# Copying attention probabilities and the last residual into fp32r buffers by DMA, and transposing them as fp32r

## What is computed

```python
# first block: 8 heads of 64, window 128, blocks of 128 tokens
probs = softmax(concat([scores * 64 ** -0.5 + mask, sink]))[..., :-1]
out = einsum("bnhgqk,bnkhd->bnqhd", probs, vw)
# second block, two layers: 8 heads of 64, chunks of 64, 8 chunks to the left
p = softmax(where(valid, scores + bias, -1e30))
out = einsum("bnhqk,bnkhd->bnqhd", p, vb)
# end: the residual stream x plus the last projection, normalised
return rms_norm_2(x + y @ w_out, final_gain)
```

## Time and profile before

| | |
|---|---|
| Median of three runs | 1216.86 us |
| The profiled execution, its own time | 1217.13 us |
| Its span (first to last instruction) | 1215.0 us |
| PE busy | 1202.1 us, 99% |
| PEld busy | 1012.2 us, 83% |
| DVE busy | 827.8 us, 68% |
| ACT busy | 553.6 us, 46% |
| POOL busy | 385.8 us, 32% |

### The profile page before, as it was taken

How to read it: one execution, slowest core, us unless ns; L and a number is a source line. 1 busy time by engine, 2 the same in 40 slices (tenths; PEclk the granted TensorE clock), 3 DMA queues, 4 the chain that set the end, 5 groups by cost and what they waited for, 6 DMA issues and landing times.

```text
span 1215.0 us, 15012 instructions
## 1 busy us (share of the span) xinstructions
PE 1202.1 (99%) x5822; PEld 1012.2 (83%) x5822; DVE 827.8 (68%) x1520; ACT 553.6 (46%) x954; POOL 385.8 (32%) x283
## 2 busy tenths in 40 slices
PE   9999999999999999999999999999999999999997
PEld 7888888888888888888888879898888889898886
DVE  5868735466888537653569877767967866677864
ACT  6557533324444324433334566653335555643433
POOL 0035279997000000000003238775203033464200
PEclk9999999999999999999999999999999999999999
DMA  8232232322323232233223333222223332222221
GB/s 303 75 101 70 70 114 87 104 78 95 104 87 119 90 99 89 90 112 96 93 73 96 121 112 95 89 88 78 78 72 101 105 105 88 87 90 95 76 70 70
DMA packets 35911, 117.42 MB, mean 97 GB/s; under 512 B 3968, under 2 KB 4480, under 8 KB 35840
## 3 DMA queue, kind: packets, MB, share of 16 engines
q1 hardware_dynamic: 35552, 116.28, 29.6%
q10 hardware_dynamic: 288, 0.18, 0.0%
HBM read 114.35 MB, written 2.10 MB: 96 GB/s over the span
## 4 chain that ended last, share of the span: by engine, by line
PE 87%; DVE 7%; ACT 3%; issue 1%; POOL 1%; DMA 0%; SPq 0%; ACTq 0%; DVEq 0%
PE ps L284 84%; DVE RA L261 3%; DVE FA L273 2%; ACT RA L253 2%; PE ps L1415 1%; DVE FA L261 1%; POOL RA L261 1%; DVE RA L273 1%; PE ps L813 1%; ACT RA L257 1%; DMA FA<-w_units 0%; PE ps L479 0%; ACT FA L257 0%; PE ps L521 0%; POOL FA L261 0%
## 5 line engine op out<-in xcount | busy, mean ns | idle before, releaser
L284 PE MATMUL ps<-RA 128*128 128x512 f32 (+1 forms) x5470 | 1179.3, 376 | 6.4 <-DVE RA L261 4.1
L284 PEld LDWEIGHTS ps<-RA 128*128 128x128 f32 x5470 | 974.3, 189 | 188.9 <-DVE RA L261 4.8
L253 ACT ACTIVATE RA<-FA 128x1024 fp32r<-128x1024 f32 (+4 forms) x337 | 279.7, 857 | 338.7 <-PE ps L284 165.2
L261 DVE TENSOR_TENSOR RA<-FA,RA 128x1024 fp32r<-128x1024 f32 (+6 forms) x302 | 322.3, 1078 | 161.7 <-ACT RA L253 157.5
L261 POOL TENSOR_TENSOR FA<-FA 128x512 f32<-128x512 f32 (+1 forms) x88 | 116.4, 1324 | 443.3 <-ACT FA L257 417.3
L277 POOL TENSOR_SCALAR FA<-FA 128x256 f32<-128x256 f32 (+3 forms) x117 | 147.2, 1270 | 161.9 <-DVE FA L281 160.8
L273 DVE SCALAR_TENSOR_TENSOR FA<-ps,FA 128x512 f32<-128x512 f32 (+3 forms) x137 | 98.1, 721 | 90.2 <-PE ps L284 44.9
L261 POOL TENSOR_TENSOR RA<-FA,RA 128x512 fp32r<-128x512 f32 (+1 forms) x37 | 70.4, 1914 | 111.2 <-ACT RA L253 111.2
L258 ACT ACTIVATE FA<-FA 128x512 f32<-128x512 f32 (+4 forms) x109 | 60.3, 555 | 97.1 <-DVE FA L1385 76.0
L273 DVE SCALAR_TENSOR_TENSOR FA<-FA 128x4 f32<-128x4 f32 (+4 forms) x166 | 84.4, 515 | 20.6 <-ACT FA L253 7.9
L257 ACT ACTIVATE FA<-ps,FA 128x512 f32<-128x512 f32 x56 | 38.1, 684 | 108.3 <-PE ps L284 108.3
(11 more groups left out here) (43 smaller groups left out, 274.9 us busy)
## 6 DMA issues: line engine op xcount, KB each, us to landing
FA<-w_units SPq DMA_DIRECT2D x189, 512.0 KB, 3.5
FA<-rel SPq DMA_DIRECT2D x16, 256.0 KB, 3.2
FA<-w_units SPq DMA_DIRECT2D x8, 384.0 KB, 3.0
FA<-x SPq DMA_DIRECT2D x8, 256.0 KB, 5.7
FA<-x_rows SPq DMA_DIRECT2D x4, 512.0 KB, 9.2
FA<-dmat SPq DMA_DIRECT2D x8, 256.0 KB, 3.3
out<-FA SPq DMA_DIRECT2D x8, 256.0 KB, 2.2
FA<-w_units SPq DMA_DIRECT2D x2, 256.0 KB, 4.2
```

Source lines behind the costliest of these rows:

```text
L253: return lambda eng: eng.activation(dst, src, ACT.Copy)
L261: return lambda eng: eng.tensor_tensor(dst, a, b, op)
L284: return lambda e: e.matmul(dst, a, b, start=start, stop=stop_)
```

## The change

The 248 transposes of lines 813, 1415 and 1628 get operands and results of type fp32r, while the data keep their bits:

- A new buffer `UA` holds an identity of type fp32r (`identr`, one ACT copy) and 1280 columns `TP` for probabilities.
- First block: after `pn.s.3` a DMA `pm.s` on SP's queue copies the stage's probabilities from `P1` to a new double buffer `PR` in `RA` (128x1024, 512 KB; in stages 0 and 1 128x4x128, 256 KB). The transposes wait for the copy, and the probabilities' buffer is free from the copy on.
- Second block: after the two `pn` of a half a DMA copies its 640 columns (320 KB) to `TP`, and the five transposes wait for that.
- End: four DMAs `hm.t` copy the residual of 128 tokens each (128x8x128, 512 KB in pieces of 512 bytes) into unused places of `RA`. They are issued after units 1 to 4, and their transposes come after units 4 to 7.
- The early gate tiles move to other columns of `FA`, which makes room.

```diff
+        def turn(dst, src):
+
+            return lambda e: e.transpose(dst.bitcast(F32R), src, U(TI, 128))
...
+            a_move(s)
+
+        def a_move(s):
+
+            n, g = stages[s]
+            nk = 256 if n else 128
+            cut = lambda ap: steps(ap, [[256, 4], [1, nk]])
+            dma(f"pm.{s}", [f"pn.{s}.3"] + take(f"pr.{s % 2}"), cut(Rf(PR + 1024 * (s % 2), 1)),
+                cut(F(P1 + 1024 * (s % 2), 1)), f"pm{s % 2}")
+            for t in range(4):
+                free(f"p1.{s % 2}.{t}", f"pm.{s}")
...
-                    after = [f"pn.{s}.3"] + take(f"bank{b}") if t == 0 else []
-                    T(f"pT.{s}.{j}" if t == 3 else None, after, lambda e, t=t, j=j, b=b: e.transpose(
-                        bank(b, 128, 128 * t), F(pb + 256 * t + 128 * j, 128), F(ID, 128)))
...
+                    after = [f"pm.{s}", "identr"] + take(f"bank{b}") if t == 0 else []
+                    T(f"pT.{s}.{j}" if t == 3 else None, after,
+                      turn(bank(b, 128, 128 * t), R(pr + 256 * t + 128 * j, 128)))
...
+                    dma(f"{pre}pm.{h}.{half}", [f"{pre}pn.{h}.{i}" for i in pair] + take(f"tp{half}"),
+                        U(TP + 640 * half, 640).bitcast(F32), F(PB + 640 * half, 640), f"pm{half}")
+                    for i in pair:
+                        free(f"pb{i}", f"{pre}pm.{h}.{half}")
...
+                        after = [f"{pre}pm.{h}.{half}"] + take(f"bank{b}") if j == 0 else []
+                        T(f"{pre}pT.{h}.{i}" if j == i else None, after,
+                          turn(bank(b, 128, 128 * j), U(TP + hoff[i] + 128 * j, 128)))
...
+            hm = [K2P, K2P + 1024, RVH, RVH + 1024]
+
+            def copy_residual(t):
+
+                dma(f"hm.{t}", ["1s.7.1" if t < 2 else "1o.11"], steps(Rf(hm[t], 1), [[128, 8], [1, 128]]),
+                    steps(F(H + 128 * t, 1), [[512, 8], [1, 128]]), f"hm{t}")
...
+                        T(f"xt.{t}.{half}" if k == 3 else None, [f"hm.{t}"] + take(f"bank{b}") if k == 0 else [],
+                          turn(bank(b, 128, 128 * k), R(hm[t] + 512 * half + 128 * k, 128)))
...
+                if 1 <= k < 5:
+                    copy_residual(k - 1)
```

More of the change, by code:

```diff
@@ L50 @@
 XBH, XBL = Z + 22528, Z + 26624
+PR = Z + 26368
 R_COLS = Z + 30720
+TP, TI = 0, 1280
+T_COLS = TI + 128
 RAW, H = 0, 3072
@@ L64 @@
 QT = Y + 256
-TG = Y + 6760
-F_COLS = TG + 2048
+TG0, TG1 = COS, Y + 5632
+F_COLS = Y + 6760
 X0H, X0L = Z + 16896, Z + 20992
@@ L224, in two_blocks_kernel @@
         FA = ctx.enter_context(nc.sbuf_tensor("FA", [128, F_COLS], F32))
+        UA = ctx.enter_context(nc.sbuf_tensor("UA", [128, T_COLS], F32R))
         PS = [ctx.enter_context(nc.psum_tensor(f"ps{i}", [128, 512], F32)) for i in range(8)]
@@ L236, in F, with U @@
             return FA[p0:p1, c:c + n]
+        def U(c, n=512):
+            return UA[0:128, c:c + n]
+        def turn(dst, src):
+            return lambda e: e.transpose(dst.bitcast(F32R), src, U(TI, 128))
         def steps(ap, dims):
@@ L751, in two_blocks_kernel @@
         staggered([k_evacuate(), normal(2), q_split(2)])
-        gate = early_gate("ga", 0, 1, TG, 0)
+        gate = early_gate("ga", 0, 1, TG0, 0)
         staggered([v_evacuate(), normal(3), q_split(3), gate])
-        gate = early_gate("gc", 0, 2, TG + 512, 8)
+        gate = early_gate("gc", 0, 2, TG0 + 512, 8)
         staggered([normal(4), gate])
-        gate = early_gate("ga", 1, 3, TG + 1024, 0)
+        gate = early_gate("ga", 1, 3, TG1, 0)
         staggered([normal(5), gate])
-        gate = early_gate("gc", 1, 4, TG + 1536, 8)
+        gate = early_gate("gc", 1, 4, TG1 + 512, 8)
         staggered([normal(6), gate, normal(7)])
@@ L811, in a_transpose @@
                 for t in range(4):
-                    after = [f"pn.{s}.3"] + take(f"bank{b}") if t == 0 else []
-                    T(f"pT.{s}.{j}" if t == 3 else None, after, lambda e, t=t, j=j, b=b: e.transpose(
-                        bank(b, 128, 128 * t), F(pb + 256 * t + 128 * j, 128), F(ID, 128)))
-            for t in range(4):
-                free(f"p1.{s % 2}.{t}", f"pT.{s}.{1 if n else 0}")
+                    after = [f"pm.{s}", "identr"] + take(f"bank{b}") if t == 0 else []
+                    T(f"pT.{s}.{j}" if t == 3 else None, after,
+                      turn(bank(b, 128, 128 * t), R(pr + 256 * t + 128 * j, 128)))
+            free(f"pr.{s % 2}", f"pT.{s}.{1 if n else 0}")
         def a_split(s):
@@ L877, in a_slot @@
             in_step([soft, evac, fin])
+        A("identr", ["ident"], copy(U(TI, 128), F(ID, 128)))
         slot = 0
@@ L967, in tga @@
         def tga(m):
-            return TA + 512 * (m % 2) if m % 4 > 1 else TG + 1024 * (m % 2)
+            return TA + 512 * (m % 2) if m % 4 > 1 else (TG0, TG1)[m % 2]
         def tgc(m):
-            return TC + 512 * (m % 2) if m % 4 > 1 else TG + 1024 * (m % 2) + 512
+            return TC + 512 * (m % 2) if m % 4 > 1 else (TG0, TG1)[m % 2] + 512
         def merge(m, ba, bc):
@@ L1413, in half_turn @@
                     for j in range(i + 1):
[L1414 to L1417, removed]
+                        after = [f"{pre}pm.{h}.{half}"] + take(f"bank{b}") if j == 0 else []
+                        T(f"{pre}pT.{h}.{i}" if j == i else None, after,
+                          turn(bank(b, 128, 128 * j), U(TP + hoff[i] + 128 * j, 128)))
+                if h < 8:
+                    free(f"tp{half}", f"{pre}pT.{h}.{(0, 1)[half]}")
             def half_split(h, half):
@@ L1626, in to_token_major @@
                     for k in range(4):
-                        T(f"xt.{t}.{half}" if k == 3 else None, take(f"bank{b}") if k == 0 else [],
-                          lambda e, b=b, k=k, half=half: e.transpose(
-                              bank(b, 128, 128 * k), F(H + 512 * (4 * half + k) + 128 * t, 128), F(ID, 128)))
+                        T(f"xt.{t}.{half}" if k == 3 else None, [f"hm.{t}"] + take(f"bank{b}") if k == 0 else [],
+                          turn(bank(b, 128, 128 * k), R(hm[t] + 512 * half + 128 * k, 128)))
                     dst = F(xtm[t] + 512 * half)
```

2 lines of the change are left out of this document (1 added, 1 removed).

## The result

The changed kernel takes 1213.89 us, the median of 12 runs (1213.45 to 1214.32), against 1216.80 us of the kernel before in the same comparison (12 runs, 1216.28 to 1217.59). The ratio is 0.9976, with a 95% interval from 0.9968 to 0.9984. That is 2.9 us or 0.24% less. The forecast was 1207.7, 9.1 us less. The direction was right and the size was not, and the measured time lies in the upper half of the stated range, where the prediction had put "a part of the gain".

What follows compares the result with a forecast made beforehand. PE's instruction costs were taken as the bound. Span 1215.0 - 12.6 (transposes) + 2.4 (group ends) + 0.7 + 0.3 (copies) = 1205.8 us; with 2.13 around it and 0.27 off for the median, 1207.7. Range 1205.0 to 1220.0.

Steps and rivals of the forecast that it cites:

- a part of the gain: Transposes: an fp32r pass costs something between 58 and 109 ns; at 84, 1212.8 us; chance 0.08.
- What bounds the kernel: Whole kernel: PE, busy 1202.1 of 1215.0 us, so only cheaper PE work gains and PE waits lose.
- What a transpose costs now: The 248 fp32 transposes: 109 ns each, bound by a double pass, load of 50 hidden; 27.0 us of PE.
- What it costs after: The transposes in fp32r: 58 ns each, from a pass of 58 and a load of 50.
- The term of 12.6 us: Gain on the transposes, 248 x (109 - 58) ns.
- How the load was read: Matmuls after an idle engine, load exposed: fp32r 0.50 instead of 0.39 us, load 110 ns; transpose 0.32 instead of 0.27, load 50.
- The end of a group: Behind each of 44 transpose groups the next fp32r load shows, 44 x 0.055 = 2.4 us lost.
- The rule on loads: Transposes: a load takes columns over 1.2 GHz, 107 ns for 128, so they would gain only 0.5 us in all.
- rival 1: Transposes gain nothing: pass stays 109 ns or load takes 110; 1217.9 to 1218.8 us; chance 0.28 with copies on time.
- The copies: The 44 added DMAs: landing 3.5 us for 512 KB, 2.9 for 320 KB; stage 5 0.6 us late.
- Stage 7 and the residual: Waits for copies: 0.1 us at stage 7 of the first attention, 0.3 for the tightest residual copy at the end.
- The slower rival: Copies land late, PE waits at groups' first transposes, which gain nothing; 1223.6 us at 4.5 us landing; chance 0.18.

Runs made afterwards that it cites:

- The probes: The changed kernel with rows of ten equal transposes or matmuls, varied in shape and type, added behind its last matmul; 1244.95 us in one run.

## Why the prediction was wrong

**What bounds the kernel**: right. PE is still busy 99%, what its instructions save comes out of the time, and what it waits goes in.

**What a transpose costs now**: right. 109 ns, bound by a double pass, with a shorter load hidden behind it. The probes show both halves of it.

**What it costs after**: this is the step that failed. The prediction took "58" for the distance of the fp32r transposes, from a pass of 58 and a load of 50. The pass was right (60). The load was not: "the short load is seen on transposes alone, so it goes with the mode". It goes with both: 62 ns or less in fp32 transpose mode, 85 in fp32r transpose mode, 111 plain. The term of 12.6 us should have been 248 x 24 = 6.0, and somewhat more, since the first two of most groups cost only 61 and 65. The value of 85 stood between the two ends that the text had kept (50 and 110), which is why the range held the time. The case that came true, "a part of the gain", had a chance of 0.08: the text had that case for the pass only, and treated the load as one of two values. Between two measured relatives of a new operation a value in the middle deserved more.

**How the load was read**: from a matmul after an idle engine, 0.32 against 0.27 us. For plain fp32r this reading agrees with the distance in a row (110 and 111). For the fp32r transposes it does not: at stage 5, after the wait, the first lasts 282 ns against 222 with its load covered, so 60 ns show, but in a row each load costs 85. The changed kernel's own durations of line 249 (ns, min/median/max) have all three:

```profile
L249 PE MATMUL ps<-UA,RA x88: 218/248/282, 81.7 to 1182.7; 128*128 128x128 f32 x88
```

**The end of a group**: right in kind, mis-sized. 72 ns were measured where 55 were written, 0.8 us more over 44 groups.

**The rule on loads** from the Trainium skill, "TensorE: Matmul & The Clock Gate", section "LDWEIGHTS (loading the stationary operand)", divides the columns by 1.2 GHz; the estimate from it, 107 ns for 128 columns, is met by the plain fp32r loads (111). It is not met in transpose mode, where fp32r needs 85 and fp32 at most 62. By the rule the change would have gained nothing; the groups gained 4.5 of the 10.2 us that I expected, and part of my rival 1 was in the right direction: the load, not the pass, became the bound.

**The copies**: the place was right, and the number partly by luck. The one wait is where it was expected, at stage 5, 0.75 us for 0.6. But the forecast took the room from the kernel before (2.91 us from POOL's end) and a landing of 3.5. The copy landed after 3.2 us, and the room had shrunk to about 2.4: PE had gained some 0.6 us in the five groups ahead of it, while POOL's scaling ended at 117.95 us instead of 117.85. A kernel's own gain ahead of a fixed producer turns into waiting, and the prediction left that out; with the full gain that it forecast, the wait would have been longer by some 0.7 us (32 transposes x 51 ns less 5 x 55, against the 0.6 measured). In the kernel with copies and fp32 transposes, where PE gains nothing, the wait was 0.26. The copies of 512 KB in the first attention land in 3.1 to 3.3 us (3.5 expected), those of 320 KB in 2.5 (2.9), and no wait appears in the second block. Stage 7 and the residual, for which 0.1 and 0.3 us were set, do not wait in the changed kernel. The weight loads behind the copies did come later without harm: ACT waits for them 1.1 us in three cases, where it was 0.9 in two. The load of the relative bias lands after 3.9 instead of 3.2 us, which is hidden as well.

**The slower rival** (late copies) did not occur: no copy of probabilities in the changed kernel's profile needed the 3.8 us from which it would have (3.6 at most). The copies of the residual did, with 5.3 to 7.5 us, but had over 7 us of room in the forecast and at least 1.3 us to spare in the profile. The copies alone cost 0.8 us.

With the measured terms the sum of the prediction reads 1216.8 - 4.5 + 1.0 = 1213.3 us, 0.6 below the measured time.

## What to carry to other kernels

When PE is the bound, a matmul's cost in a row was here the larger of two things, the load of one operand and the pass of the other (for the first two of a row nearly the pass alone), and a change of type moves both, not always the same way. To price a form that the trace does not have, take neither relative for granted: ten of them in a row behind the kernel's end, with one operand halved, tell load from pass in one run. And a copy by DMA between two engines costs nothing where the room between writer and reader is above its landing (3.2 us for 512 KB and 2.5 for 320 KB here). Take off that room what the change itself gains ahead of it, where the writer does not come earlier too. Only the tightest stage pays, and when it is relieved, the next ones do: of 0.9 us won at stage 5, 0.2 were left two stages on. And before a difference of some tenths of a us between two profiles is explained, find the place where it arises and look whether a second profile of the same kernel has it.

## What the runs showed of the hardware

- Transposes of four-byte data by TensorE: in fp32 109 ns each, bound by the pass of the identity; in fp32r 85, bound by the load of the data, with a pass of 60. Fewer data columns shorten only the fp32r form, a smaller identity (with as many fewer rows) only the fp32 form.
- The first two fp32r transposes behind a wide matmul cost 61 and 65 ns, but each group pays 72 ns behind its last one. In all a group of four gained 72 ns, one of five 86, one of eight 160. A single fp32r transpose between 512-wide matmuls costs 61 + 58 ns.
- An fp32 transpose right behind a row of fp32r ones costs 131 ns; when the two alternate, a pair costs 61 + 112.
- A copy within SBUF landed no later than a load of its size: 2.3 to 2.8 us for 256 KB and 2.5 for 320 KB, where loads of 256 KB took 2.8 to 3.9; 3.2 for 512 KB, where loads took 3.5. In pieces of 512 bytes a copy of 512 KB took 5.3 us, and three queued ones came 1.8 us apart.
